# Hybrid encoder block on one core: the first expert's rows from one-hot products, a last stage shared by TensorE, and later weights for the fifth buffer

## The reference, cut to what matters

```python
h = rmsnorm(x, norm_ffn_g)
gp, gi = top_1(softmax(h @ w_group_router + b_group_router))            # 4 groups
ew, ei = top_2(softmax(expert_logits(h) of group gi))                   # 2 of its 8 experts
weights = gp * ew / sum(ew)
for e in range(32):                                                     # width 256 each
    hid = silu(h @ w_exp_gate[e]) * (h @ w_exp_up[e])
    out = out + combine[:, e:e + 1] * (hid @ w_exp_down[e])
x = x + out
return rmsnorm(x, norm_final_g)
```

## Time and profile before

| what | value |
|---|---|
| median of 3 runs | 888.8 us (888.28 to 889.62) |
| the profiled execution's own time | 885.0 us |
| its span | 883.1 us |
| PE busy | 770.2 us, 87% |
| DVE, ACT, POOL busy | 359.8, 244.3, 294.4 us |
| mean granted TensorE clock | 0.957 of full |
| HBM read and written | 157.57 and 13.04 MB |
| chain that ended last | PE 54%, DMA 25%, DVE 9%, issue 5%, ACT 4%, POOL 2% |

### The profile page before, as it was taken

The page is one execution under the profiler, slowest core; times in us unless marked ns, Lnnn a source line. Parts: engine busy times, 40 slices in busy tenths (PEclk is TensorE's granted clock), DMA queues, the critical chain, the costliest instruction groups (busy, mean ns, idle before and its releaser), DMA issues.

```text
span 883.1 us, 14710 instructions
## 1 busy us (share of the span) xinstructions
PE 770.2 (87%) x5715; PEld 631.0 (71%) x5715; DVE 359.8 (41%) x767; ACT 244.3 (28%) x421; POOL 294.4 (33%) x256
## 2 busy tenths in 40 slices
PE   5999999899899979999996998957999999987830
PEld 5888798788788857788885877845777777756610
DVE  6478760562763861236513513551121212121117
ACT  4333242112212746522213446320111111101012
POOL 3823444422530243034442434323333333322102
PEclk9999999999999989999997999967999999999975
DMA  9755504202220431374492455384999999999943
GB/s 256 138 102 108 111 10 96 48 5 46 49 48 2 98 94 36 62 193 94 95 283 50 102 187 212 144 333 173 394 392 392 398 388 390 386 389 389 368 164 153
DMA packets 71513, 162.84 MB, mean 184 GB/s; under 512 B 18876, under 2 KB 44300, under 8 KB 63272
## 3 DMA queue, kind: packets, MB, share of 16 engines
q1 hardware_dynamic: 63920, 150.66, 53.5%
q0 software_dynamic: 5696, 10.50, 3.5%
q10 hardware_dynamic: 1848, 1.02, 0.7%
HBM read 157.57 MB, written 13.04 MB: 193 GB/s over the span
## 4 chain that ended last, share of the span: by engine, by line
PE 54%; DMA 25%; DVE 9%; issue 5%; ACT 4%; POOL 2%; SPq 1%; DVEq 0%; POOLq 0%; ACTq 0%
PE bank L977 14%; DMA arena<-in_w_exp_up 13%; PE bank L984 11%; PE bank L986 10%; PE bank L985 10%; DMA ring<-in_w_exp_up 8%; PE bank L1305 3%; DMA ring<-in_w_cq 1%; PE bank L1315 1%; DVE xres L1955 1%; DVE arena L1664 1%; DMA arena<-y_half 1%; PE bank L1187 1%; DMA h_rows<-hT 1%; ACT w_high L1360 1%
## 5 line engine op out<-in xcount | busy, mean ns | idle before, releaser
L984 PE MATMUL bank<-h_hi,w_high 128*128 128x512 f32 x296 | 123.2, 416 | 2.3 <-DVEq L543 2.0
L807 POOL TENSOR_TENSOR ring_low<-ring,w_high 128x2048 fp32r<-128x2048 f32 (+1 forms) x16 | 71.6, 4477 | 149.5 <-ACT w_high L1360 132.9
L1305 PEld LDWEIGHTS bank<-arena,hT 128*64 128x64 f32 x1728 | 99.7, 139 | 25.4 <-issue 21.5
L985 PE MATMUL bank<-h_lo,w_high 128*128 128x512 f32 x296 | 116.5, 394 | 0.0
L1305 PE MATMUL bank<-arena,hT 128*64 128x128 f32 x1728 | 103.6, 279 | 8.2 <-DMA arena<-in_w_exp_up 7.4
L807 POOL TENSOR_TENSOR w_low<-ring,w_high 128x2048 fp32r<-128x2048 f32 x14 | 64.4, 4599 | 78.9 <-ACT w_high L1360 77.0
L1928 DVE SCALAR_TENSOR_TENSOR rt<-rt,bank 128x128 f32<-128x128 f32 x32 | 9.2, 288 | 181.7 <-ACT rt L1565 181.7
L1360 ACT ACTIVATE w_high<-ring 128x2048 fp32r<-128x2048 f32 (+1 forms) x32 | 58.8, 1838 | 66.6 <-PE bank L986 30.7
L984 PEld LDWEIGHTS bank<-h_hi,w_high 128*128 128x128 f32 x296 | 56.3, 190 | 15.2 <-DVEq L543 2.3
L986 PE MATMUL bank<-h_hi,ring_low 128*128 128x512 f32 x168 | 66.7, 397 | 0.0
L985 PEld LDWEIGHTS bank<-h_lo,w_high 128*128 128x128 f32 x296 | 56.2, 190 | 9.6
(11 more groups left out here) (281 smaller groups left out, 1373.1 us busy)
## 6 DMA issues: line engine op xcount, KB each, us to landing
arena<-in_w_exp_gate SPq DMA_DIRECT2D x27, 1024.0 KB, 11.9
arena<-in_w_exp_up SPq DMA_DIRECT2D x27, 1024.0 KB, 16.9
arena<-in_w_exp_down SPq DMA_DIRECT2D x27, 1024.0 KB, 19.5
ring<-in_w_in SPq DMA_DIRECT2D x33, 512.0 KB, 6.6
ring<-in_w_exp_gate SPq DMA_DIRECT2D x5, 1024.0 KB, 12.9
ring<-in_w_exp_up SPq DMA_DIRECT2D x5, 1024.0 KB, 16.9
ring<-in_w_exp_down SPq DMA_DIRECT2D x5, 1024.0 KB, 19.7
xres<-in_x SPq DMA_DIRECT2D x8, 512.0 KB, 7.1
```

Source lines behind the costliest of these rows:

```text
L807: after(pool.tensor_tensor(low, full, high, ALU.subtract), w_lo)
L984: pe.matmul(o, l_hi, r_hi, start=(n == 0), stop=False)
L985: pe.matmul(o, l_hi, r_lo, start=False, stop=False)
L1305: ins = pe.matmul(bank[CAP * half:CAP * half + CAP, 1, P * n:P * n + P], xgT[:, x, kk, :], w[:, kk, P * half:P * half + P], start=(kk == 0 ...
```

## The change

Five things are changed.

1. **The order of the last jobs** and their banks: `pos` of a tile and the first transposes of tile 3 come earlier; transposes of `co`'s first half wait for that half alone; the last turn's second half is copied by DVE instead of ACT.
2. **The last tile's normed rows** are written by ACT right behind the square and the root, not behind the router product, into a place of their own, and ACT, not POOL, issues their store (semaphore `last_hrow_out`).
3. **The fifth buffer's weights** (`load_part(4, i)`) are asked for on SP behind that store's landing. The load of the final gain goes from ahead of the loop to behind the last expert's weights.
4. **The first expert's rows** aren't gathered. Four new jobs `("g0", t)` on PE multiply the normed rows of tile t (16 matmuls, 128 x 128 weights, 64 columns) by a one-hot table `first_at[t]` and sum in bank 0. POOL makes the table for tiles 0 to 2 (three operations of 128 x 64 each), DVE for tile 3 (two operations). DVE multiplies bank 0 by the gain ahead of the loop. PE's and DVE's first turn of six experts is written out, and in expert 0 the turn of the next rows comes behind the down product. Five matmuls of 256 columns into spare banks are added (3 ahead of `pos` of tile 3, 2 ahead of the first expert).
5. **The last stage**: tiles go in the order 2, 0, 3, 1, each load of `y_half` has its own semaphore, and tiles 2 and 3 are summed by PE in PSUM (identity times `xres`, then a diagonal of the token weights times each `y`); ACT squares from there. The roots take POOL's power (two calls) and one Newton step of DVE in place of DVE's three steps from a bit trick. DVE finishes all four tiles; ACT's and POOL's scaling passes are gone.

```diff
-    jobs += [("co", 3, 0), ("rt", 2), ("pos", 1), ("co", 3, 1), ("pos", 2), ("hT", "ffn", 3, 0), ("hT", "ffn", 3, 1), ("rt", 3), ("pos", 3)]
-    jobs += [("ls",), ("most",)]
+    jobs += [("co", 3, 0), ("pos", 1), ("rt", 2), ("hT", "ffn", 3, 0), ("co", 3, 1), ("g0", 0), ("hT", "ffn", 3, 1), ("pos", 2), ("rt", 3)]
+    jobs += [("g0", 1), ("pos", 3), ("g0", 2), ("ls",), ("g0", 3), ("most",)]
...
+LATE_BANKS = {"g0": 0, "ls": 6, "most": 3}
+FILL = {("pos", NT - 1): 3, "turned": 2}
+LAST_TURN = ("hT", "ffn", NT - 1, 1)
+        LAST_ORDER = (2, 0, 3, 1)
...
             load_part(2, 2)
             load_part(3, 1)
+            sp.wait_ge(last_hrow_out, 16)
             for i in range(3):
                 load_part(4, i)
-            sp.dma_start(gain_out, norm_final_g...).then_inc(gains_in, 16)
...
+                if k == "pos" and c < NT - 1:
+                    pool.wait_ge(list_ready, c + 1)
+                    after(pool.tensor_scalar(first_at[:, c, :], at_slot[0][:, c, :], oh[0][:, c, 0:1], None, ALU.mult))
+                    after(pool.tensor_scalar(second_at, at_slot[1][:, c, :], oh[1][:, c, 0:1], None, ALU.mult))
+                    after(pool.tensor_tensor(first_at[:, c, :], first_at[:, c, :], second_at, ALU.add), first_slots)
...
+                if k == "g0":
+                    t = job[1]
+                    pe.wait_ge(*((first_slots, t + 1) if t < NT - 1 else (last_slots, 1)))
+                    pe.wait_ge(hrow_ready, t + 1)
+                    for kk in range(KD):
+                        ins = pe.matmul(o[:, CAP * kk:CAP * kk + CAP], normed_row[t]...[:, kk, :], first_at[:, t, :],
+                                        start=(t == 0 and kk == 0), stop=(t == NT - 1), skip_group_check=True)
...
+            for b in range(UNROLL):
+                expert(0, b, lambda: turn_rows(...), turn_last=(b == 0))
+            with pe.Fori(1, TURNS, 1) as i:
...
+            pe.wait_ge(weights_ready, 1)
+            for t in (2, 3):
+                for half in range(2):
+                    pe.matmul(sum_banks(t)[:, half, :], ident, xres[:, t, 512 * half:512 * half + 512], start=True, stop=False)
+            for _ in range(4):
+                pe.matmul(bank[:, 3, :], ident, cst[:, 0:512], start=True, stop=True)
+            for t in (2, 3):
+                for j in range(2):
+                    pe.wait_ge(y_in[t][j], 16)
+                    for half in range(2):
+                        ins = pe.matmul(sum_banks(t)[:, half, :], y_weight[j][:, t - 2, :], y_rows(t, j)[:, 512 * half:512 * half + 512], start=False, stop=(j == 1))
+                ins.then_inc(summed, 1)
...
+                    after(nc.scalar.activation(junk, xres[:, t, :], ACT.Square, accum_out=squares[:, 10 + t:11 + t]), squared)
+                    if t == NT - 1:
+                        act.wait_ge(ffn_rstd, NT)
+                        copy(normed_row[t], xres[:, t, :], hrow_ready, scale=rstd[:, 10 + t:11 + t])
+                        act.dma_start(h_rows[t * P:(t + 1) * P, :], normed_row[t]).then_inc(last_hrow_out, 16)
...
+            add(0)
+            roots(0, 2)
+            add(1)
+            finish(0, 2)
+            roots(2, 4)
+            finish(2, 4)
```

More of the change, by code:

```diff
@@ L963, in _ @@
                     pool.wait_ge(more_out, n * 16 + 16)
[L964 to L967, removed]
+            for n in range(2):
+                pool.wait_ge(var_ready, n + 1)
+                after(pool.tensor_tensor(rstd[:, 14 + 2 * n:16 + 2 * n], var[:, 2 * n:2 * n + 2], neg_half.to_broadcast([P, 2]), ALU.pow), root_ready)
         @block.tensor
@@ L1281, in _ @@
                     continue
+                for _ in range(FILL.get(job, 0)):
+                    pe.matmul(bank_of(job)[:, 0:256], ident, cst[:, 0:256], start=True, stop=True)
                 emit(job if job[0] != "sc" else ("sc", job[1], job[2] - 2)).then_inc(done, 1)
+            spare = jobs[-BANKS]
+            job_empty(pe, spare)
+            for _ in range(FILL["turned"]):
+                pe.matmul(bank_of(spare)[:, 0:256], ident, cst[:, 0:256], start=True, stop=True)
             for job in held.values():
-                job_empty(pe, job)
+                if job[0] not in LATE_BANKS:
+                    job_empty(pe, job)
             def turn(b, s):
@@ L1960, in _, with roots @@
-            add(2)
-            rms(14, 2, scale_ready)
-            add(3)
-            rms(16, 2)
-            for t in (2, 3):
-                after(stt(out=xres[:, t, :], in0=xres[:, t, :], scalar=rstd[:, 14 + t:15 + t], in1=gain_out, op0=ALU.mult, op1=ALU.mult), fin_ready)
+            def roots(a, b):
+                n = slice(14 + a, 14 + b)
+                v, y, y2 = var[:, a:b], rstd[:, n], newton[:, a:b]
+                dve.wait_ge(squared, 14 + b)
+                after(ts(v, squares[:, n], 1.0 / D, EPS, ALU.mult, ALU.add), var_ready)
+                dve.wait_ge(root_ready, b // 2)
+                after(tt(y2, y, y, ALU.mult))
+                after(stt(out=y2, in0=y2, scalar=-0.5, in1=v, op0=ALU.mult, op1=ALU.mult))
+                after(stt(out=y, in0=y2, scalar=1.5, in1=y, op0=ALU.add, op1=ALU.mult))
@@ new lines, in finish @@
+            def finish(a, b):
+                for place in range(a, b):
+                    t = LAST_ORDER[place]
+                    halves = lambda tile: tile.rearrange("p (h c) -> p h c", h=2)
+                    source = sum_banks(t) if t >= 2 else halves(xres[:, t, :])
+                    after(stt(out=halves(xres[:, t, :]), in0=source, scalar=rstd[:, 14 + place:15 + place], in1=halves(gain_out), op0=ALU.mult, op1=ALU.mult), fin_ready)
+            for j, t in itertools.product(range(2), (2, 3)):
+                ins = ts(y_weight[j][:, t - 2, :], ident, wgt[j][:, t:t + 1], None, ALU.mult)
+                after(ins, weights_ready if (j, t) == (1, 3) else step["dve"])
```

142 lines of the change are left out of this document (92 added, 50 removed).

## The result

The median of the changed kernel is **882.8 us** (four runs, 881.2 to 883.8), against 888.5 us for four runs of the kernel before on the same chip (887.8 to 889.6): a ratio of 0.9937, with a 95% interval of 0.9921 to 0.9954. That is 5.6 us faster, between 4.1 and 7.0. The forecast was 873.1 us with a range up to 880.8. So the sign is right and two thirds of the gain are missing. The profiled execution took 881.2 us with a span of 879.4, against 883.1 before; the forecast span was 867.4, so 12.0 us are missing in the span.

A forecast was written before the change was run, and what follows sets the result against it. Weight transfers bound the expert stream, whose start waits for expert 0's gate and up. Routing 11.4 us less 1.0 given back makes 10.4; with 5.3 in the last stage, 15.7 off 888.8 gives 873.1 us, range 870 to 880.8.

The forecast's parts named there:

- the price of `g0`: PE's routing: each `g0`, priced like the router product, takes 1.9 us, or 3.3 at the lower clock.
- Rival (a): Routing on PE: the clock falls to 0.50 and costs 7.5 us together, giving 880.6 us; chance 0.16.
- the sign that I had named for being wrong: Routing: the clock row showing 0.50, where the forecast expected 1.00 from 577 to 600 us.
- The added matmuls: PE's routing: 256 columns each, between 0.25 and 0.5 us, taken as 0.4; three lie in PE's wait for DVE.
- The last store: Store of the last normed rows: takes 3.0 us and lands at 586.4 us instead of 595.8.
- The hold: SP's wait before the fifth buffer's loads: costs nothing unless expert 0 is ready before 595 us.
- The second gate and up: Expert loop: ends 9.3 us behind the first instead of 7.3, while the stream needs 8.9; 0.5 us given back.
- The stream's rate: Stream of expert weights: stays at 8.9 us per expert as before.
- Rival (b): Weight stream doesn't follow: last store lands at 595.8 as before and SP holds all weights; 879.0 us, chance 0.09.
- The last stage: From the first load back to DVE's last operation: 22.4 us instead of 27.7, a gain of 5.3 us.
- rival (c): Last stage gains only 1.6 us because PE runs at the lower clock: 876.8 us, chance 0.07.
- rival (d): First six experts: written-out PE code waits behind weights, 7.8 us each time, and the sign turns: 896.5 us, chance 0.05.

The follow-up runs named there:

- products_only: The changed kernel with only the `g0` products reading contiguous weight columns, rows written as before, so the first expert's values differ: 872.6 us, ratio 0.9823.
- contig: The changed kernel with normed rows written column block by column block, so `g0` and the turns of gathered rows read contiguous words: 871.9 us, ratio 0.9798.
- contig_again: The same kernel as contig, run once more in another set: 873.2 us, ratio 0.9831.
- contig_fill_router: The changed kernel with contiguous normed rows and two more added matmuls ahead of the last router product: 873.3 us, ratio 0.9835.

## Why the prediction was wrong

**The step that failed** is the price of `g0`: "`g0` is 16 matmuls with 128 x 128 weights like the router product, so 1.9 us, or 3.3 at the lower clock". It measured 3.80, 4.03, 4.04 and 4.07 us. Size and count were those of the router product, the way its weights are read was not: every eighth word, 335 ns a load instead of 192 at full clock. That it is the read, and no other feature of `g0`, is shown by products_only, which changes the read alone: 872.6 us, and the path of contig, 21.0 us. A hint was to be had: the Trainium skill, Advanced Engine Details and Errata, "SBUF Cachelines", says that reads which touch another 16-byte line each time pay a penalty. Every eighth 4-byte word is such a read, and the 335 against 192 ns at full clock agree with it; at 0.50 (335 against 333) the traces show no penalty.

The step came in four times, and on the way down its effect grew. Each line is the end of a step, forecast and measured in the kernel after:

| step ends | forecast | measured | late by |
|---|---|---|---|
| turn of tile 3 and DVE's copy | 580.2 | 581.9 | 1.7: `g0` of tile 0 stands before it |
| router product | 582.2 | 585.7 | 3.5: clock 0.50, 3.60 us instead of 1.9 |
| DVE's choice | 585.5 | 589.2 | 3.7: 3.3 us, as forecast |
| at-slot rows | 587.6 | 594.5 | 6.9: `g0` of tile 1 ends at 589.5, then the three added matmuls, 2.7 us, that the sum hid in DVE's chain |
| list product | 589.9 | 598.3 | 8.4: `g0` of tile 2 |
| `g0` of tile 3 | 591.8 | 602.4 | 10.6 |
| gate and up begin | 592.9 | 604.6 | 11.7: two added matmuls 2.05 us, booked at 0.8 |
| gate and up end | 596.6 | 608.9 | 12.3: partly at 0.50, 4.42 us |

So PE had no wait left in which to hide anything. That was also my second fault in kind: work booked as hidden in another engine's wait (`g0` of tile 1, three added matmuls) had a cover of 3.3 us and measured 6.5 in the chain (3.83 and 2.67). With the price of a contiguous read the same plan comes near: contig and contig_again measured 871.9 and 873.2 us, the forecast 873.1. That it is so near is in part luck. Their path is 21.0 us instead of 18.9, the span 870.6 and 871.4 instead of 867.4, and in both the add began later (580.5 and 579.7) than the 578.1 I summed from. The sum also added the 3.8 us by which the profiled execution of the kernel before lay under the median; in contig the profiled execution lies 0.5 us above it and in contig_again at it. The two errors, 3 to 4 us each, cancel.

**Rival (a), the clock,** came true as well (0.50 at 582 us, and again from 596), as did the sign that I had named for being wrong, 0.50 in the routing. By its price, 7.5 us, it would have given 880.6. In the kernel after, the router product (3.6 for 1.9), the list (1.9 for 1.1) and gate and up (4.4 for 3.8) together lost some 3 us to it, the five added matmuls 2.3 (4.92 for 1.51 and 1.11). `g0` lost next to nothing more, because at full clock its slow loads held it at 3.8 to 4.0 us. The two causes can't be added up apart: with contiguous loads `g0` loses 1.7 us at 0.50 (3.65 for 1.98), and slow loads pushed the router product behind the first fall and stood where the clock fell a second time. "Against: PE's list is now filled" was a wrong argument: at 596 us the clock fell with the list full of slow loads. In contig_fill_router, with two more matmuls in the list and contiguous loads, it held.

**The added matmuls** cost 0.50 to 0.56 us each at full clock (in contig_fill_router three in 1.51, two in 1.11) and 1.0 at 0.50 (2.87 and 2.05 in the kernel after; each shows as two records). I took 0.4 between bounds of 0.25 and 0.5, so the upper bound was a little low, and the low clock wasn't in it. Nor was it in the sum that they pay only if they bring the clock back.

**The last store** landed at 587.8, not 586.4 (4.4 us, not 3.0), and it didn't matter. **The hold** costs nothing, as forecast, and gives nothing; that was tested with contiguous rows only. **The second gate and up** came 9.5 us behind the first, forecast 9.3. **The stream's rate** stayed: T0 − request is 245.1 us after and 244.1 before. Rival (b) is out by the same rows: SP's request waits for gate and up, and the store isn't late. **The last stage** gained 5.6 us in the profile, forecast 5.3; rival (c) is out. Of rival (d), code that waits behind weights, no run shows a sign: behind the second expert the requests come 7.2 us apart (618.58, 625.77), as before.

## What to carry to other kernels

Before a product takes its price from another of the same shape, compare how the two read their weights: here a stride of eight words doubled it at full clock, and one rearrangement where the rows are written took the ratio from 0.9937 to 0.9798 and 0.9831. Work hidden in another engine's wait must be summed against the length of that wait, all of it together. Matmuls added for the clock pay only if they bring it back before the long products. Of the kernels run here, contig is the one to keep: its interval lies below those of both kernels. The hold on SP could go without loss.

## What the runs showed of the hardware that I had not expected

A weight load of 128 x 128 fp32 takes 335 ns from every eighth word and 192 ns from words in a row at full clock. At 0.50 it takes 335 and 333 ns, so there the stride costs nothing. Eight such matmul calls take 3.80 us at 1.00 and 4.03 at 0.50 with the stride, 1.89 to 2.00 and 3.65 without: slow loads set their pace, not the clock.

The granted clock fell to 0.50 at 596 us while PE was shown as busy in every microsecond since 592, in slow loads; in contig, in the same order of work with contiguous rows, it stayed at 1.00 from 592 us through gate and up. A busy share of 1.00 in the profile isn't a promise of the full clock. What exactly the chip counts, these runs don't settle.
